# Neighbourhood attention: plain fp32 scores on unsplit queries and keys

## What is computed

```python
qg = q.reshape(B, rows, GRID_W, NA_HEADS, NA_DIM) * (NA_DIM ** -0.5)
s = jnp.einsum('bchd,bjkhd->bhcjk', q_r, k_r, preferred_element_type=jnp.float32)
s = jnp.where(col_in[None, None, :, None, :], s + bias[None], -jnp.inf)
p = jax.nn.softmax(...)
```

## Time and profile before

| | |
|---|---|
| median of three runs | 1710.65 us (1709.75 to 1714.07) |
| profiled execution | 1709.23 us |
| its span, first to last instruction | 1707.6 us |
| mean granted TensorE clock | 0.973 of full |
| instructions | 20141 |
| HBM read, written | 160.93 MB, 28.41 MB |

### The profile page before, as it was taken

One profiled execution on the slowest core, in us unless ns is written; L12 is line 12 of the kernel. 1 busy time (PEld: TensorE's weight loads), 2 busy tenths in 40 slices (PEclk: granted clock), 3 DMA queues, 4 the chain that ended last, 5 costly groups with the idle time before them and its releaser, 6 DMA issues. The chain is left out here.

```text
span 1707.6 us, 20141 instructions
## 1 busy us (share of the span) xinstructions
PE 1568.1 (92%) x7518; PEld 1173.2 (69%) x7518; DVE 876.9 (51%) x1549; ACT 697.0 (41%) x1172; POOL 379.6 (22%) x440
## 2 busy tenths in 40 slices
PE   3869998999999998999995999899999999899997
PEld 0457884567877776777884788356777777677786
DVE  2253224575588544776324332467558743677522
ACT  1033333665443344443333243466453342544333
POOL 3001300442220003564100220134212000356410
PEclk9889999999999999999998999999999999999998
DMA  9927842121433351114332974112133235111434
GB/s 339 387 62 161 228 124 74 34 63 53 135 99 87 91 150 56 38 38 123 106 117 90 198 202 129 44 34 90 50 111 113 86 98 148 38 47 38 146 93 147
DMA packets 245566, 190.70 MB, mean 112 GB/s; under 512 B 51854, under 2 KB 221145, under 8 KB 242904
## 3 DMA queue, kind: packets, MB, share of 16 engines
q1 hardware_dynamic: 244440, 186.69, 37.4%
q0 software_dynamic: 1024, 2.67, 0.6%
HBM read 160.93 MB, written 28.41 MB: 111 GB/s over the span
## 5 line engine op out<-in xcount | busy, mean ns | idle before, releaser
L333 DVE TENSOR_TENSOR w_lo<-at,w_hi 128x1024 fp32r<-128x1024 f32 x158 | 199.2, 1261 | 388.0 <-ACT w_hi L326 387.8
L326 ACT ACTIVATE w_hi<-at 128x1024 fp32r<-128x1024 f32 x158 | 166.3, 1054 | 136.8 <-PE ps L530 126.3
L528 PE MATMUL ps<-h_e_hi,w_hi 128*128 128x512 f32 x480 | 190.9, 398 | 7.9 <-DVE w_lo L333 7.9
L530 PE MATMUL ps<-h_e_hi,w_lo 128*128 128x512 f32 x480 | 187.0, 390 | 0.0
L529 PE MATMUL ps<-h_e_lo,w_hi 128*128 128x512 f32 x480 | 187.0, 390 | 0.0
L528 PE MATMUL ps<-h_a_hi,w_hi 128*128 128x512 f32 x400 | 159.3, 398 | 12.1 <-ACT at L755 9.1
L530 PE MATMUL ps<-h_a_hi,w_lo 128*128 128x512 f32 x400 | 156.8, 392 | 0.0
L529 PE MATMUL ps<-h_a_lo,w_hi 128*128 128x512 f32 x400 | 156.7, 392 | 0.0
L1115 POOL TENSOR_SCALAR at<-at,at 128x512 f32<-128x512 f32 x128 | 87.0, 692 | 164.0 <-DVE at L1052 164.0
L528 PEld LDWEIGHTS ps<-h_e_hi,w_hi 128*128 128x128 f32 x480 | 90.1, 188 | 43.8 <-DVE at L1266 11.7
L530 PEld LDWEIGHTS ps<-h_e_hi,w_lo 128*128 128x128 f32 x480 | 90.1, 188 | 19.2
(11 more groups left out here) (273 smaller groups left out, 3129.0 us busy)
## 6 DMA issues: line engine op xcount, KB each, us to landing
at<-w_in SPq DMA_DIRECT2D x117, 512.0 KB, 4.2
at<-w_ada SPq DMA_DIRECT2D x16, 1536.0 KB, 14.2
at<-w_out SPq DMA_DIRECT2D x48, 512.0 KB, 4.0
z_kept<-at SPq DMA_DIRECT2D x32, 256.0 KB, 2.3
at<-z_kept SPq DMA_DIRECT2D x32, 256.0 KB, 2.8
at<-rpb_pad SPq DMA_DIRECT2D x32, 224.0 KB, 4.4
t_masked<-at SPq DMA_DIRECT2D x16, 448.0 KB, 4.7
at<-t_masked SPq DMA_DIRECT2D x16, 448.0 KB, 3.3
```

The lines of the kernel that those rows point to most:

```text
L326: act.activation(whi[:, b % PAIRS], wring[:, b % SLOTS], ACT.Copy).then_inc(sem("w_hi"), 1)
L333: dve.tensor_tensor(wlo[:, b % PAIRS], wring[:, b % SLOTS], whi[:, b % PAIRS].bitcast(F32), ALU.subtract)\
L528: pe.matmul(o, stationary[0], moving[0], start=first, stop=False)
L530: return pe.matmul(o, stationary[1], moving[0], start=False, stop=final)
```

## The change

Queries and keys of the neighbourhood heads are kept as one F32 array each, where there were two F32R arrays. ACT writes all queries, DVE all keys, each in one operation from PSUM; the separate operation for the lower part is gone. PE's wait on the banks goes by two new semaphores. In `score_quad` there is one plain fp32 product per head and block, in place of three F32R ones; the alternation of the two heads stays.

```diff
-    naq = pair("naq", N0, N0 + 4 * T, n=4)
-    nak = pair("nak", N0 + 8 * T, N0 + 12 * T, n=4)
+    naq = chunks(take(4 * T, at=N0), T)
+    nak = chunks(take(4 * T, at=N0 + 8 * T), T)
...
-                        pe.wait_ge(sem("naqk_lo"), b - B_NAQK + 1)
+                        if b < B_NAQK + 4:
+                            pe.wait_ge(sem("naq_done"), b - B_NAQK + 1)
+                        else:
+                            pe.wait_ge(sem("nak_done"), b - B_NAQK - 3)
...
-                    if B_NAQK <= b < B_NAV:
-                        n = b - B_NAQK
-                        dve.wait_ge(sem("naqk_hi"), n + 1)
-                        o = (naq if n < 4 else nak)
-                        if n < 4:
-                            dve.scalar_tensor_tensor(naq[1][:, n], ps(b % 4), NA_D ** -0.5, naq[0][:, n].bitcast(F32),
-                                                     ALU.mult, ALU.subtract).then_inc(sem("naqk_lo"), 1)
-                        else:
-                            dve.tensor_tensor(nak[1][:, n - 4], ps(b % 4), nak[0][:, n - 4].bitcast(F32), ALU.subtract)\
-                                .then_inc(sem("naqk_lo"), 1)
+                    if B_NAQK + 4 <= b < B_NAV:
+                        n = b - B_NAQK - 4
+                        dve.wait_ge(sem("blk_done"), b + 1)
+                        dve.tensor_copy(nak[:, n], ps(b % 4)).then_inc(sem("nak_done"), 1)
                     dve_split(dve, b + PAIRS)
...
-                    if B_NAQK <= b < B_NAV:
+                    if B_NAQK <= b < B_NAQK + 4:
                         n = b - B_NAQK
                         act.wait_ge(sem("blk_done"), b + 1)
-                        if n < 4:
-                            act.activation(naq[0][:, n], ps(b % 4), ACT.Copy, scale=NA_D ** -0.5).then_inc(sem("naqk_hi"), 1)
-                        else:
-                            act.activation(nak[0][:, n - 4], ps(b % 4), ACT.Copy).then_inc(sem("naqk_hi"), 1)
+                        act.activation(naq[:, n], ps(b % 4), ACT.Copy, scale=NA_D ** -0.5).then_inc(sem("naq_done"), 1)
...
-                    for s, (a, b) in enumerate(((0, 0), (0, 1), (1, 0))):
-                        for e in range(2):
-                            r = 64 * e
-                            last = pe.matmul(ps(s_bank(j + e) + m), naq[a][r:r + 64, n, at:at + P], nak[b][r:r + 64, n],
-                                             start=(s == 0), stop=(s == 2))
-                            if m == 1 and s == 2:
-                                last.then_inc(sem("c_s"), 1)
+                    for e in range(2):
+                        r = 64 * e
+                        last = pe.matmul(ps(s_bank(j + e) + m), naq[r:r + 64, n, at:at + P], nak[r:r + 64, n], start=True, stop=True)
+                        if m == 1:
+                            last.then_inc(sem("c_s"), 1)
```

## The result

| | before | after |
|---|---|---|
| median | 1709.87 us (16 runs) | 1713.06 us (16 runs, 1709.09 to 1716.53) |
| profiled execution | 1709.23 | 1716.53 |
| span | 1707.6 | 1714.9 |

The ratio is 1.0018, interval 1.0009 to 1.0026: 3.1 us slower (1.5 to 4.4), within 0.3%. The range, 1712 to 1724, held the median, 1.1 us above its lower end. The forecast of +5.1 us is over the upper end of the interval.

A forecast was written before the change was run, and what follows sets the result against it. PE, busy 92% of the span, was taken to bound the kernel. Score products +5.1 us and projection 0, on the three-run median of 1710.65, gave 1715.8 us; its own range 1713 to 1719, the 8-in-10 range 1712 to 1724.

The forecast's parts named there:

- What bounds: Whole kernel: PE, busy 92% of the span; in the neighbourhood half, PE and the chain through the scores set the pace.
- Two chains: Neighbourhood half, beside PE: one through scores and DVE's copy, one through exponentials and reciprocals with 0.07 us to spare; period 6.12.
- The lower bound: Score products: if a product were a single record, 0.54 us less a group, 0.07 paid out, 1.1 us off.
- rival 2: Score groups: a 64-row product takes fewer than two records; -1.1 us, 1709.6 us; chance 0.04.
- Part 1: Score products (L977): plain products, side by side on row halves, make a group 1.90 us, +0.32 each, 16 groups, +5.1 us.
- The joined evidence: Score products: plain products share the array by columns, split ones by row halves; so plain ones on row halves run side by side.
- Part 2: Projection splits: DVE loses 11.0 and gets 5.4 us, ACT loses 4.8; none on the path, value 0 (bounds 0 to +5.4).
- Sum: Whole kernel: +5.1 us on the profiled 1709.23 us is 1714.3; against the median of three runs, 1715.8 us.
- 1: Score groups: row halves don't share the array in plain fp32, 8 records in sequence; +33 us, 1743 us; chance 0.07.
- 3: Score groups: records start in program order, five slots instead of four; +12.0 us, 1722.7 us; chance 0.07.
- 4: Projection: a gain there, needing PE to wait for splits; a time of 1705 us or less; chance 0.01.
- the 0.3% line: Whole kernel: about 5.1 us, what a measurement can tell from no change; the +5.1 forecast lies on it.

The follow-up runs named there:

- two_products: Kernel before with two F32R score products per head and block instead of three (queries' upper by keys' lower left out); median 1707.75 us, -2.2 by the ratio.
- one_product: Kernel before with a single F32R score product per head and block (upper by upper) instead of three; median 1709.29 us, -0.7 by the ratio.
- evict_only: Changed kernel's single evictions in F32R, with three F32R score products all from the upper parts; against the kernel before 0.0 us by the ratio, median 1710.02 us.
- again: The changed kernel run once more with no edit; ratio to the kernel before 1.0012 (1.0001 to 1.0023), median 1712.51 us.
- scores_only: Kernel before, evictions and splits kept, scores as plain fp32 products on the upper parts only; +2.6 us by the ratio, median 1714.17 us.

## Why the prediction was right, and where not

- *What bounds.* Right. Two chains and PE close within 0.07 us of each other; shown by two_products and one_product, whose periods stop at 6.05. The lower bound and rival 2's price (-1.1) missed the first group of each pass, which pays its gain in full: with that the price is 2 x 0.54 + 14 x 0.07 = 2.1 us, an estimate.
- *Part 1.* Right to 0.02 us: group 1.92 (forecast 1.90), period 6.45 (6.44), stage +5.24 (+5.1). The joined evidence (columns for plain products, rows for split ones) held.
- *Part 2.* Right in its value: evict_only 0.0. DVE's busy time did not fall by the 5.6 us that part 2 gives it: it is 876.9 before and 876.7 after, and of that 3.5 us are the splits at L333, which took longer (199.2 to 202.7). PE had no idle time there all the same.
- *Sum.* Here it was off by 2 us. The step is the sum "+ 5.1 us on the profiled execution's 1709.23 us": the stage does carry it whole, but the rest of the span isn't constant to 2 us. The prediction took the rest for fixed, and held the spread of executions for noise that leaves the median alone. The medians of changed and before show that it doesn't. The size of the term "all else" was taken as 0 and measured as -2.1 (interval -3.7 to -0.8) in the first 16 executions, and -3.2 and -2.6 in again and scores_only. Most of it goes with the granted clock, as shown above. Of the 2.7 us between the forecast of 1715.8 and the measured 1713.06 another 0.8 is the base: the median of three runs was 1710.65, that of 16 is 1709.87.
- *The rivals.* 1 and 3 fell with the first row of the profile (8 records in 1.99 us), 2 with the record count, 4 with evict_only.
- *The chances.* "Same" at 0.44 and "slower" at 0.54 came from putting the forecast on the 0.3% line. The missing 2 us decided for "same", the verdict that had the smaller chance, and the range held by its lower part, which had been kept wide for the spread of the runs. Nothing in the working foresaw that the time would move by less than the stage, so that the range held it is in part luck.

## What to carry to other kernels

A plain fp32 product takes 0.86 us for 512 columns where three F32R ones take 0.69, and 64-row halves share the array in both, so leaving the split out pays only where the split's own operations are on the path; here they were under 5.5 us blocks of PE work. Before making a stage's largest item cheaper, follow the chain that does not hold it: here it allowed 0.07 us a period, and a change of order gave 0.6. And a stage can be forecast to 0.01 us a period while the time of the kernel still differs by 2 us, so read the stage from the profile and the verdict from many runs, and set the granted clocks beside the times.

## What had not been expected of the hardware

- The granted clock over the span differs between kernels whose stage differs by a few us: 0.9747 (16 and 11 executions) against 0.9723 (35) and 0.9724 (11), with no low clock in the changed stage of either. The same 3149 records outside the stage took 741.1 to 749.5 us, with 27 to 48 us of them at the low level.
- With one head's products all ahead of the other's in the program, the two halves of the array still start together (both at 361.47 us), so a loop's order over row halves costs nothing here.
